# Moving the last up pieces and the turned copies in the expert units of 64 slots

## The reference

```python
def swiglu(x, w_gate, w_up, w_down):
    return (jax.nn.silu(x @ w_gate) * (x @ w_up)) @ w_down

def moe_swiglu(xn, w_router, we_gate, we_up, we_down):
    logits = (xn @ w_router).astype(jnp.float32)
    top_v, top_i = lax.top_k(logits, TOP_K)                 # 2 of 8 experts
    top_w = jax.nn.softmax(top_v, axis=-1)
    gates = jnp.sum(jax.nn.one_hot(top_i, N_EXPERTS) * top_w[..., None], axis=-2)
    y = jnp.zeros_like(xn)
    for e in range(N_EXPERTS):
        y = y + gates[..., e:e + 1] * swiglu(xn, we_gate[e], we_up[e], we_down[e])
    return y
```

## Time and profile before

| what | value |
|---|---|
| median of three runs | 1412.25 us |
| profiled execution, its own time | 1413.07 us |
| its span, first to last instruction | 1411.3 us |
| TensorE busy | 1393.1 us, 99% |
| VectorE busy | 1182.7 us, 84% |
| ScalarE busy | 1026.7 us, 73% |
| granted TensorE clock, mean | 0.997 |
| DMA | 443.13 MB, mean 314 GB/s |

### The profile page before, as it was taken

The page is one execution under the profiler, slowest core; times in us unless marked ns, Lnnn a source line. Parts: engine busy times, 40 slices in busy tenths (PEclk is TensorE's granted clock), DMA queues, the critical chain, the costliest instruction groups (busy, mean ns, idle before and its releaser), DMA issues.

```text
span 1411.3 us, 18791 instructions
## 1 busy us (share of the span) xinstructions
PE 1393.1 (99%) x6747; PEld 1162.3 (82%) x6747; DVE 1182.7 (84%) x1501; ACT 1026.7 (73%) x1317; POOL 86.3 (6%) x110
## 2 busy tenths in 40 slices
PE   8999999999999999999999999999999999999997
PEld 8998888888897878888878888878888887888886
DVE  6968655554489699989999989999998999998998
ACT  6665544444479387888888888887878888878885
POOL 1000000000010000000030001012001003000000
PEclk9999999999999999999999999999999999999999
DMA  8554465555262599999999999999999999999996
GB/s 303 169 194 150 160 228 179 178 180 190 77 228 72 213 327 407 379 366 386 402 403 405 402 382 392 391 406 398 409 401 375 388 403 403 404 402 358 411 403 237
DMA packets 143223, 443.13 MB, mean 314 GB/s; under 512 B 8894, under 2 KB 20508, under 8 KB 143132
## 3 DMA queue, kind: packets, MB, share of 16 engines
q1 hardware_dynamic: 139772, 429.89, 80.7%
q0 software_dynamic: 3328, 12.06, 3.0%
q10 hardware_dynamic: 32, 0.01, 0.0%
HBM read 434.06 MB, written 7.86 MB: 313 GB/s over the span
## 4 chain that ended last, share of the span: by engine, by line
PE 87%; DVE 10%; ACT 2%; DMA 1%; issue 0%; SPq 0%; DVEq 0%; ACTq 0%
PE bank L597 83%; DVE w_lo L1962 8%; PE bank L1242 1%; DMA raw<-in_w_mem_kv_dram 1%; DVE act_f L2694 0%; ACT w_hi L1410 0%; PE bank L942 0%; PE bank L609 0%; ACT xr L1545 0%; DVE aT_hi L2704 0%; DVE xT_lo L2656 0%; PE bank L1206 0%; PE bank L1044 0%; DVE xT_lo L2006 0%; PE bank L1094 0%
## 5 line engine op out<-in xcount | busy, mean ns | idle before, releaser
L1962 DVE TENSOR_TENSOR w_lo<-raw,w_hi 128x1024 fp32r<-128x1024 f32 (+2 forms) x832 | 952.6, 1197 | 130.9 <-ACT w_hi L1410 125.7
L1410 ACT ACTIVATE w_hi<-raw 128x1024 fp32r<-128x1024 f32 (+2 forms) x832 | 833.8, 1041 | 231.9 <-PE bank L597 181.9
L597 PE MATMUL bank<-w_hi,xT_hi 128*128 128x512 f32 (+3 forms) x1358 | 527.2, 388 | 3.2 <-DVE w_lo L1962 1.8
L597 PE MATMUL bank<-w_hi,xT_lo 128*128 128x512 f32 (+3 forms) x1358 | 520.6, 383 | 0.0
L597 PE MATMUL bank<-w_lo,xT_hi 128*128 128x512 f32 (+3 forms) x1358 | 519.9, 383 | 0.0
L597 PEld LDWEIGHTS bank<-w_hi,xT_hi 128*128 128x128 f32 x1358 | 255.1, 188 | 53.3 <-issue 5.4
L597 PEld LDWEIGHTS bank<-w_hi,xT_lo 128*128 128x128 f32 x1358 | 254.9, 188 | 49.1
L597 PEld LDWEIGHTS bank<-w_lo,xT_hi 128*128 128x128 f32 x1358 | 255.3, 188 | 46.2
L597 PE MATMUL bank<-w_hi,aT_hi 128*128 128x512 f32 x544 | 217.8, 400 | 3.4 <-DVE w_lo L1962 3.4
L597 PE MATMUL bank<-w_lo,aT_hi 128*128 128x512 f32 x544 | 214.8, 395 | 0.0
L597 PEld LDWEIGHTS bank<-w_hi,aT_hi 128*128 128x128 f32 x544 | 102.2, 188 | 31.2 <-issue 4.3
(11 more groups left out here) (396 smaller groups left out, 736.3 us busy)
## 6 DMA issues: line engine op xcount, KB each, us to landing
raw<-in_we_gate_dram SPq DMA_DIRECT2D x112, 1024.0 KB, 9.1
raw<-in_we_up_dram SPq DMA_DIRECT2D x112, 1024.0 KB, 9.8
raw<-in_we_down_dram SPq DMA_DIRECT2D x112, 1024.0 KB, 10.3
raw<-in_w_gate_dram SPq DMA_DIRECT2D x14, 1024.0 KB, 5.1
raw<-in_w_up_dram SPq DMA_DIRECT2D x14, 1024.0 KB, 5.1
raw<-in_w_down_dram SPq DMA_DIRECT2D x14, 1024.0 KB, 4.8
raw<-in_w_in_dram SPq DMA_DIRECT2D x16, 768.0 KB, 5.3
raw<-in_w_out_dram SPq DMA_DIRECT2D x8, 1024.0 KB, 5.7
```

Source lines behind the costliest of these rows:

```text
L597: return pe.matmul(o, a, b, start=start, stop=stop, skip_group_check=True, **kw)
L1410: act.activation(split_piece(w_hi, c, shape, half), raw_piece(c, shape, half), ACT.Copy).then_inc(hi_ready, 1)
L1962: dve.tensor_tensor(split_piece(w_lo, c, shape, half), raw_piece(c, shape, half), F(split_piece(w_hi, c, shape, half)), ALU.subtract).then ...
```

## The change

In the units of 64 slots only, the four up pieces of the last strip move behind the first four down pieces of the last wide strip. In the new numbering 0 to 3 are gate, 4 to 7 down (first half), 8 to 11 up, 12 to 15 down (second half), 16 to 19 as before. The fetches on SyncE's queue follow the same order. TensorE makes turn 0 before piece 0 and turn 1 before piece 2 (before: ahead of pieces 4 and 8). ScalarE copies them after its pieces 1 and 4 (before: 8 and 13), VectorE after its pieces 1 and 5 (before: 7 and 12). The turn of the last strip's halves moves from ahead of piece 12 to ahead of piece 14. ScalarE copies these halves ahead of its pieces 16 and 17 instead of behind them.

```diff
@@ expert (SyncE)
+                    if narrow:
+                        down_rows(c, NF - 3 + n, more)
+                        c += 2
-                for n, f in enumerate((NF - 3, NF - 2, NF - 1)):
+                for n, f in enumerate((NF - 1,) if narrow else (NF - 3, NF - 2, NF - 1)):
                     down_rows(c + 2 * n, f, more)
@@ unit (TensorE)
+                if narrow:
+                    e_turn(n, t, 0)
+                    e_in(c, 0, more, inside=lambda: e_turn(n + 1, t + 1, 1))
+                    e_down(c + 2, more, t, False, True, blocks=range(FB))
+                    e_in(c + 4, 1, more)
+                    e_down(c + 4, more, t, False, True, inside=next_turned, blocks=range(FB, 2 * FB), at=FB + 2)
@@ unit (ScalarE)
-                    pieces(33, 48, m, lp)
+                    pieces(33, 42 if narrow and i == WIDE - 2 else 48, m, lp)
+                if narrow:
+                    e_high(t, 0, True)
+                    pieces(p + 2, p + 5)
+                    e_high(t + 1, 1, True)
+                    pieces(p + 5, p + 8)
+                    e_silu(C_MOE + SMALL + 2, more, n + 2, 1)
+                    pieces(p + 8, p + 16)
...
+                if narrow:
+                    pieces(p + 16, p + 18)
@@ unit (VectorE)
-                    pieces(37, 48, m)
+                    pieces(37, 42 if narrow and i == WIDE - 2 else 48, m)
...
                 e_low(t, 0, narrow)
+                if narrow:
+                    pieces(p + 2, p + 6)
+                    e_low(t + 1, 1, True)
+                    pieces(p + 6, p + 14)
+                    e_product(C_MOE + SMALL + 6, more, n + 2, 1)
+                    pieces(p + 14, p + 16)
```

More of the change, by code:

```diff
@@ L423, in _, with expert @@
                     fetch(c, sizes[c], src)
-            def expert(e, more, c0=C_MOE):
+            def expert(e, more, narrow=False, c0=C_MOE):
                 gate, up = (w.rearrange("e (j k p) n -> j e p k n", j=4, p=P) for w in (we_gate1, we_up1))
@@ L449, in expert @@
                 c = c0 + SMALL
-                for w in small:
+                for n, w in enumerate(small):
                     for j in range(2):
@@ L460, in _ @@
             for u in range(1, NE):
-                expert(sp.value_load(order_i[0:1, u:u + 1], min_val=0, max_val=NE - 1), FFN_CHUNKS * u)
+                expert(sp.value_load(order_i[0:1, u:u + 1], min_val=0, max_val=NE - 1), FFN_CHUNKS * u,
+                       u in NARROW_UNITS)
             sp.wait_ge(sem("units_known"), 1)
@@ L1208, in gathered_turned, with e_in @@
                         last.then_inc(sem("gather_psum"), 1)
-            def e_in(c, which, more):
+            def e_in(c, which, more, inside=None):
                 for j in range(4):
+                    if inside and j == 2:
+                        inside()
                     pe.wait_ge(lo_ready, 2 * c + j + 1 + 2 * more)
@@ L1287, in e_down_end, with e_down @@
                     last.then_inc(piece_used, 1)
-            def e_down(c, more, t, start, narrow, inside=None):
+            def e_down(c, more, t, start, narrow, inside=None, blocks=range(2 * FB), at=FB):
                 terms = down_terms(narrow)
-                for j in range(2 * FB):
-                    if inside and j == FB:
+                for j in blocks:
+                    if inside and j == at:
                         inside()
@@ L1342, in unit @@
                 pe.wait_ge(sem("esilu_done"), n + 2)
[L1343 to L1346, removed]
                 def next_turned():
@@ L1351, in next_turned @@
                         gathered_turned(u + 1)
-                e_down(c + 4, more, t, False, narrow, inside=next_turned)
+                if narrow:
[4 more added lines that the diff above has]
+                    e_down(c + 4, more, t, False, True, inside=next_turned, blocks=range(FB, 2 * FB), at=FB + 2)
+                else:
+                    e_in(c, 0, more)
+                    e_turn(n, t, 0)
+                    e_in(c + 2, 1, more)
+                    e_turn(n + 1, t + 1, 1)
+                    e_down(c + 4, more, t, False, False, inside=next_turned)
                 e_down_end(c + 8, more, u, last, narrow)
@@ L1878, in unit @@
                     e_high(t0 + 2 * i + 1, 1, narrow)
-                    pieces(33, 48, m, lp)
+                    pieces(33, 42 if narrow and i == WIDE - 2 else 48, m, lp)
                 p, n, t = 2 * SMALL, n0 + NF - 3, t0 + NF - 3
[L1881 to L1886, removed]
+                if narrow:
[5 more added lines that the diff above has]
+                    pieces(p + 8, p + 16)
+                else:
+                    pieces(p + 8, p + 9)
+                    e_high(t, 0, False)
+                    e_silu(C_MOE + SMALL + 2, more, n + 2, 1)
+                    pieces(p + 9, p + 14)
+                    e_high(t + 1, 1, False)
+                    pieces(p + 14, p + 18)
                 for b in range(2):
@@ L2755, in unit @@
                 e_low(t, 0, narrow)
[L2756 to L2759, removed]
+                if narrow:
[4 more added lines that the diff above has]
+                    pieces(p + 14, p + 16)
+                else:
+                    pieces(p + 8, p + 13)
+                    e_product(C_MOE + SMALL + 4, more, n + 2, 1)
+                    e_low(t + 1, 1, False)
+                    pieces(p + 13, p + 17)
                 for b in range(2):
@@ L2762, in unit @@
                     low_part(2 * b, 2, B[(6, 7)[b]], narrow).then_inc(sem("eaT_half"), 1)
-                pieces(p + 17, p + 18)
+                pieces(p + 16 if narrow else p + 17, p + 18)
                 if not last:
```

## The result

| | before | changed |
|---|---|---|
| median of 7 runs, us | 1413.05 (1411.88 to 1413.48) | 1418.56 (1415.84 to 1419.18) |
| profiled execution, us | 1413.07 | 1417.38 |
| its span, us | 1411.3 | 1415.6 |

The ratio is 1.0041, with a 95% interval of 1.0032 to 1.0051. The change makes the kernel 5.5 us slower; 5.1 was forecast. The median forecast was 1417.3, within 1413.0 to 1419.7.

A forecast was written before the change was run, and what follows sets the result against it. At narrow units' ends TensorE's work and VectorE's full list were taken as the bounds. Four units at 1.47 us less 0.75 gave +5.1 us on 1412.25, so 1417.3 us, range 1413.0 to 1419.7.

The forecast's parts named there:

- Steps 1, 2, 4 and 5: VectorE's new waits per narrow unit: first copy 0.36, piece 2 0.66, product 0.21, piece 16 0.24 us.
- the sum: The steps' waits add 1.47 us per narrow unit; four units, less 0.75 in unit 5, give 5.1 us.
- step 5: ScalarE waits for the last strip's turned halves before splitting piece 16; VectorE waits 0.24 us, bounds 0 and 0.5.
- Step 3: ScalarE's second copy, after turn 1: ready when ScalarE reaches it, so no wait and cost 0.
- Unit 5: Its VectorE waits for a split and a late first copy go, taking 0.75 us off; it ends as unit 1.
- Unit 7: The last narrow unit: the same 1.47 us of added waits as in the other narrow units.
- The transfers: Chunk fetches: slots come free up to 1.5 us later, cost 0; upper end 1.47 us more per unit.
- This is all TensorE has to win: TensorE's breaks at the ends of units 1, 3, 5 and 7, 4.2 us in all.
- bound by TensorE from its second piece on: The wide unit after each narrow one: TensorE limits it, so none of the narrow unit's loss is given back.
- Interleaving wins: Rival: even demand closes TensorE's breaks ahead of piece 18; -4.2 us, 1408.0; chance 0.06.
- The waits stay covered: Rival: copies wait on ScalarE alone and unit 5 gives its 0.7 us; 1411.5; chance 0.14.
- The transfers follow: Rival: late-freed slots bring chunks late, up to 1.47 us more per narrow unit; 1423.2; chance 0.08.

The follow-up runs named there:

- e4: The changed kernel with ScalarE's copies of the last strip's halves behind piece 17, where they stood before; 1415.93 us, ratio 1.0024 to the kernel before.
- e1: The changed kernel's order of pieces and fetches, with turn 1, copies and product placed where no engine waits for them; 1411.59 us, ratio 0.9993 to the kernel before.
- e2: The kernel before, with only ScalarE's first copy in narrow units moved three pieces sooner, behind piece 5 instead of 8; 1419.84 us, ratio 1.0057.
- e7: The kernel before, with ScalarE's first copy one piece sooner, behind piece 7, and extra TensorE transposes in unit 7's pauses; 1412.68 us, ratio 1.0002.
- e8: The kernel before, with VectorE making the tokens' low part for only 16 of 128 columns in units 2, 4 and 6; 1412.48 us, ratio 1.0007.
- e3: The change made in units 1, 3 and 5 only, unit 7 as before; 1415.74 us, ratio 1.0028 to the kernel before.
- e5: The changed kernel with ScalarE's and VectorE's copies three pieces later; 1421.32 us, ratio 1.0065 to the kernel before.
- e6: The changed kernel with two identity transposes on TensorE ahead of unit 7's waits for pieces 17, 18 and 19; 1417.16 us, ratio 1.0034 to the kernel before.

## Why the prediction was right, point by point

**Steps 1, 2, 4 and 5** hold in place, cause and size: 0.36, 0.66, 0.21 and 0.24 were forecast, 0.39, 0.62, 0.21 and 0.22 are read, and units 1 and 3 are 1.47 longer, as the sum said. Within step 5, ScalarE stood 1.98 ahead of the small copies and not some 3. Moving only these copies back wins nothing, as e4 shows, since VectorE's low parts then wait for them. Step 3's second copy does cost nothing. That it is the place of turns, copies and product and not the order of pieces, e1 and e2 show from both sides. How the 1.47 divides among the steps is read from rows; of single steps only a copy's place (e2) and step 5 (e4) were tried alone.

**TensorE's wait ahead of piece 18** is 1.22, for about 1.2 forecast. It rises by 0.74 while the unit grows by 1.47: VectorE's full list passed on the whole loss, and the idle figure at one place shows half of it. Lengths from start to start show all.

**Unit 5**: 1.47 - 0.75 = 0.72 was forecast, 0.55 measured. "I expect unit 5 to end as unit 1 will" held (113.72 and 113.71). The size was off because the 0.75 is TensorE's idle time at one place; from start to start unit 5 was 113.17 - 112.24 = 0.93 longer, and 1.47 - 0.93 = 0.54. The cause was wrong, and that the size came out near is in part luck. The prediction read the earlier trace rows as a copy that ScalarE makes late. In e7 the copy stands ahead of piece 8 and the loss stays. Late chunks made it: ScalarE waited for DMA, and each profile without the new waits in units 1, 3 and 5 has one such unit (5 in the kernel before and in e7, 1 in e1 and e8). In the changed kernel, e2, e3 and e5 no unit of the three is longer than the others, and e4's unit 1 shows how that can be: the time lost to a chunk falls into ScalarE's stand-still. In the changed kernel's unit 5 no late chunk is seen ahead of the copy at all (it stands 2.88, where 2.4 was forecast). What decides which unit gets the late chunks stays open.

**Unit 7** is the term that was too small: 1.47 forecast, 2.53 measured. The missing 1.06 is TensorE at its lower clock: in two profiles the rows show starts 0.43 apart; where the clock stays at 1.00, e4 takes 1.32 less (0.24 of it for its first pause, 0.43 instead of 0.67) and e6 0.72 less; and in e5, whose loss per unit is 2.54, unit 7 takes 2.53 more with no surplus, while e2 has the lower clock and a surplus of 1.55. The prediction counted TensorE's waits and never asked whether the clock would hold behind them. What sets the lower clock off is not shown: e5 has the same three pauses and keeps 1.00.

**The sum**: the stage grew by 6.15 against 5.1 forecast, and the medians by 5.5. Of the difference of 1.05, unit 7 makes 1.06; unit 5 takes 0.17 off, and the rest is spread over the other units. The median came out at 1418.56 against 1417.3; 0.8 of that is the kernel before, whose median of seven runs is 1413.05 and not 1412.25.

**The transfers** cost nothing that can be seen in the changed kernel, as forecast: its units 1 and 3 are longer by the sum of VectorE's waits, 1.44, to 0.03. "This is all TensorE has to win", 4.2 us, does not mean that it can be had: e8 removed the waits in units 3 and 5, and next to nothing came out (the stage is 0.27 shorter), because the chunks bound the next stretch. For the same reason "bound by TensorE from its second piece on" leaves out how near the chunks are.

**The rivals.** *Interleaving wins* is refuted by e1: with no new wait anywhere, the even demand moves the time by -0.8 us (ratio interval 0.9984 to 1.0002). The Trainium skill (Perfetto Trace Analysis, Optimization Strategy) says that interleaving may help where the most-contended engine changes over time. That has nothing to work on here, as VectorE was busy for 32.85 of 32.85 us in the stretch. *The waits stay covered* fails on ScalarE's 2.90, more than its lead. *The transfers follow* fails on the lengths: units 1 and 3 take 1.47 more and not twice that, and the wide stretches take 90.1 us in both.

No version beats the kernel before by more than the measurement can tell. e1 is the changed kernel put right, and it is level with before. A shorter list together with earlier chunks was not tried.

## What to carry to other kernels

Where an engine's list is full and another feeds it, an instruction that waits costs by what is queued behind it: subtract the feeder's lead over the full engine from its stand-still, and the rest is the loss, at every repetition. (Here ScalarE's piece 2 was to come 3.0 us later, its lead was 1.7, and 0.3 of the rest was VectorE's own small row, moved ahead of the wait: 1.0 forecast, 0.39 + 0.62 read.) A small operation in an in-order list goes behind the point where its input is ready, and moving the work that makes the input must move it too. A stage in which two engines are full should be checked for a third bound before the gain from either is counted, and an idle row's releaser should be followed one step further (VectorE waits for ScalarE, which waits for DMA) before a cause is named.

## What the runs showed of the hardware

- In the changed kernel three TensorE pauses of 0.67, 0.34 and 0.49 us within 2.3 us were followed by about 3 us at the lower clock level (mean clock 0.57 over 4 us, in both profiles), worth 1.06 us. In e5 the same three pauses at the same distances, and a fourth of 0.34, left the clock at 1.00. So did four pauses in e4 (0.43, 0.34, 0.49 and 0.34), three in the kernel before (0.33, 0.49 and 0.34) and the single pause of 1.22 us at the end of units 1, 3 and 5. In e2 pauses of 0.61, 0.49 and 0.34 were followed by the lower level (0.57 from 1405 to 1409). What parts the cases stays open.
- Where ScalarE takes 1 MB chunks as they land, they come every 2.56 us (403 GB/s in the windows), and in some stretches every 2.71 (in e7, 1147.98 to 1150.70 to 1153.41).
